# A transformer step on one Trainium2 core: modulation passes computed partly by GpSimd beside the FFN

## The reference, cut to what matters

```python
def modulation(cvec, w_mod, b_mod):              # w_mod: 1024 x 6144 for each layer
    m = jax.nn.silu(cvec) @ w_mod + b_mod
    return jnp.split(m, 6, axis=-1)              # shift, scale, gate, twice
def conv_ffn(h, w_in, conv_w, conv_b, w_out):    # d_ff = 2816
    u = h @ w_in
    up = jnp.pad(u, ((0, 0), (1, 1), (0, 0)))
    uc = up[:, :-2] * conv_w[0] + up[:, 1:-1] * conv_w[1] + up[:, 2:] * conv_w[2] + conv_b
    a, b = jnp.split(uc, 2, axis=-1)
    return (jax.nn.silu(a) * b) @ w_out
for i in range(4):
    # modulation(c_ctx, ...) for context tokens, modulation(c, ...) for latent tokens
    x = x + g1 * mixer(rmsnorm(x) * (1 + sc1) + sh1)
    x = x + g2 * conv_ffn(rmsnorm(x) * (1 + sc2) + sh2)
```

## Time and profile before

| what | value |
|---|---|
| median of three runs | 3136.57 us |
| the profiled execution, its own time | 3136.35 us |
| its span | 3134.6 us |
| PE busy | 3050.2 us, 97% |
| DVE busy | 2077.8 us, 66% |
| ACT busy | 1081.9 us, 35% |
| POOL busy | 404.3 us, 13% |
| granted TensorE clock, mean | 0.997 |

### The profile page before, as it was taken

The page is one execution under the profiler, slowest core; times in us unless marked ns, Lnnn a source line. Parts: engine busy times, 40 slices in busy tenths (PEclk is TensorE's granted clock), DMA queues, the critical chain, the costliest instruction groups (busy, mean ns, idle before and its releaser), DMA issues.

```text
span 3134.6 us, 55312 instructions
## 1 busy us (share of the span) xinstructions
PE 3050.2 (97%) x21670; PEld 2793.6 (89%) x21670; DVE 2077.8 (66%) x4004; ACT 1081.9 (35%) x2250; POOL 404.3 (13%) x392
## 2 busy tenths in 40 slices
PE   8999999999999999999999899999999989999999
PEld 6899999886699999998876699999998769999999
DVE  7766666777757666668657566656667775766665
ACT  3322223336633222324335432222223663422221
POOL 3000000133310000003237310000012231000000
PEclk9999999999999999999999999999999999999999
DMA  8533323110023332331200223233231002122211
GB/s 340 217 121 120 120 103 125 61 58 1 19 104 135 121 124 103 121 108 48 79 32 8 86 104 111 107 132 120 95 116 54 4 1 95 68 81 80 67 67 48
DMA packets 47202, 290.20 MB, mean 93 GB/s; under 512 B 4945, under 2 KB 11345, under 8 KB 13265
## 3 DMA queue, kind: packets, MB, share of 16 engines
q1 hardware_dynamic: 47058, 288.21, 25.4%
HBM read 283.98 MB, written 4.21 MB: 92 GB/s over the span
## 4 chain that ended last, share of the span: by engine, by line
PE 89%; DVE 5%; ACT 2%; DMA 2%; issue 1%; POOL 0%; SPq 0%; POOLq 0%; DVEq 0%; ACTq 0%
PE psA L2014 38%; PE psB L2014 24%; PE psA L2123 4%; PE psA L2124 3%; PE psA L2129 3%; PE psB L2031 2%; PE psB L741 2%; PE psA L811 2%; PE psA L2200 1%; DMA w_stage<-weights_dram 1%; PE psB L723 1%; PE psB L869 1%; PE psA L709 1%; PE psA L2205 1%; DVE top L1623 1%
## 5 line engine op out<-in xcount | busy, mean ns | idle before, releaser
L2014 PE MATMUL psA<-h_hi,w_hi 128*128 128x320 f32 (+1 forms) x2736 | 624.9, 310 | 2.5 <-ACT u_raw L2367 1.7
L2014 PE MATMUL psA<-h_lo,w_hi 128*128 128x320 f32 (+1 forms) x2720 | 620.4, 309 | 0.0
L2014 PE MATMUL psA<-h_hi,w_lo 128*128 128x320 f32 x2704 | 616.0, 309 | 0.0
L2554 DVE SCALAR_TENSOR_TENSOR xT<-psB,mod,xT 128x128 f32<-128x128 f32 x750 | 377.7, 546 | 221.6 <-PE psB L2014 221.6
L2014 PEld LDWEIGHTS psA<-h_hi,w_hi 128*128 128x128 f32 x2736 | 456.1, 188 | 4.2 <-ACT u_raw L2367 2.5
L2014 PEld LDWEIGHTS psA<-h_lo,w_hi 128*128 128x128 f32 x2720 | 455.1, 188 | 0.0
L2014 PEld LDWEIGHTS psA<-h_hi,w_lo 128*128 128x128 f32 x2704 | 452.1, 188 | 0.0
L2613 DVE TENSOR_SCALAR conv<-u_raw,vec_sb 128x642 f32<-128x642 f32 x176 | 108.3, 615 | 438.8 <-ACT u_raw L2367 438.8
L2431 DVE TENSOR_TENSOR w_lo<-w_stage,w_hi 128x512 fp32r<-128x512 f32 x496 | 353.0, 756 | 38.1 <-ACT w_hi L2282 38.0
L2014 PE MATMUL psB<-g_hi,wo_hi 128*128 128x320 f32 x1280 | 299.3, 315 | 0.1
L2014 PE MATMUL psB<-g_hi,wo_lo 128*128 128x320 f32 x1280 | 295.3, 312 | 0.0
(11 more groups left out here) (272 smaller groups left out, 4976.2 us busy)
## 6 DMA issues: line engine op xcount, KB each, us to landing
w_stage<-weights_dram SPq DMA_DIRECT2D x124, 1024.0 KB, 5.1
m_stage<-w_mod_dram SPq DMA_DIRECT2D x96, 1024.0 KB, 8.3
wo_stage<-w_out_dram SPq DMA_DIRECT2D x44, 1024.0 KB, 4.7
yT_dram<-xT SPq DMA_DIRECT2D x8, 322.0 KB, 2.2
xT<-xT_dram SPq DMA_DIRECT2D x1, 1544.0 KB, 9.8
xT<-xT_dram SPq DMA_DIRECT2D x1, 1032.0 KB, 6.3
w_stage<-weights_dram SPq DMA_DIRECT2D x2, 512.0 KB, 17.6
rope_raw<-rope_dram SPq DMA_DIRECT2D x3, 256.0 KB, 2.6
```

What stands on the lines that cost most here:

```text
L2014: ins = pe.matmul(o, wp, xp[:, a:b], start=first and n == 0, stop=last and n == 2)
L2554: ins = dve.scalar_tensor_tensor(out=xT[:, d, c:c + w], in0=tokens(ps, slot)[i], scalar=gate[:, d, i:i + 1], in1=xT[:, d, c:c + w], op0=AL ...
```

## The change

Passes 1 to 9 of layers 0 to 2 are divided between two engines. GpSimd takes six of the eight channels (k = 0 to 5) of m_stage: for each it multiplies the 2 x 256 weights of every partition with that partition's conditioning value, once for context and once for latent, and adds the products up in mod_acc. PE takes channels 6 and 7 as before, in the first two partition groups, and sums mod_acc over the partitions with `pick`, a matrix with one column of ones for each conditioning, into the other two groups. PE waits for GpSimd's last addition before each half (s_macc). GpSimd waits for both halves of m_stage, for the FFN norm's h (s_h), and from pass 2 on for PE's reading of the pass before. mod_acc and mod_prod lie where the norm's buffers are. The mask's semaphore is given up, its load counts on s_small.

```diff
+POOL_PASSES = 9
+POOL_KT = 6
+        mod_acc = [at(f"mod_acc{i}", [P, 2, 2 * P], F32, B_NORM + i * 2048) for i in range(2)]
+        mod_prod = [[at(f"mod_prod{k}{i}", [P, 2, 2 * P], F32, B_NORM + 4096 + (2 * k + i) * 2048) for i in range(2)]
+                    for k in range(2)]
+        pick = const("pick", [P, 2, 32])
-        s_mask = sem("mask_loaded")
+        s_macc = sem("mod_products_added")
-                dve.wait_ge(s_mask, 16)
+                dve.wait_ge(s_small, 64)
-                        sp.dma_start(mask_raw[:, :, :].rearrange("p a n -> p (a n)"), t["mask"]).then_inc(s_mask, 16)
+                        sp.dma_start(mask_raw[:, :, :].rearrange("p a n -> p (a n)"), t["mask"]).then_inc(s_small, 16)
+            # GpSimd
+            def mod_added(l, i):
+                for g in range(2):
+                    pool.wait_ge(s_m[0][g], i * 16 + 16 * (6 + MOD_PASSES * l + 1))
+                for k in range(POOL_KT):
+                    dst = mod_prod[k % 2] if k else mod_acc
+                    for c in range(2):
+                        w = m_stage[0][:, :, k, :]
+                        if k == 0 and c == 0:
+                            pool_own(pool.tensor_tensor(dst[c][:, :, :], w, cond[:, k, c:c + 1].unsqueeze(2)
+                                                        .to_broadcast([P, 2, 2 * P]), ALU.mult))
+                        else:
+                            pool_own(pool.tensor_scalar(dst[c][:, :, :], w, cond[:, k, c:c + 1], 1.0, ALU.mult, ALU.mult))
+                    for c in range(2 if k else 0):
+                        last = k == POOL_KT - 1 and c == 1
+                        pool.wait_ge(s_pown, pool_own.loop + (pool_own.n - (not last)))
+                        ins = pool.tensor_tensor(mod_acc[c][:, :, :], mod_acc[c][:, :, :], dst[c][:, :, :], ALU.add)
+                        if not last:
+                            pool_own(ins)
+                ins.then_inc(s_macc, 1)
+                if l < DEPTH - 1:                       # behind norm_pow(2 * l + 1)
+                    pool.wait_ge(s_h, KT * (2 * l + 1))
+                    mod_added(l, 1)
+                    ...
+                    with pool.Fori(2, POOL_PASSES + 1) as i:
+                        pool.wait_ge(s_mraw, i * 2 + 2 * MOD_PASSES * (l + 1))
+                        mod_added(l, i)
+            # PE
+            def mod_added(l, it, g):
+                pe.wait_ge(s_macc, it + POOL_PASSES * l)
+                for b, out in enumerate(beside(g)):
+                    n = slice(b * P, (b + 1) * P)
+                    for k in range(POOL_KT, KT):
+                        i = k - POOL_KT
+                        q = slice(32 * (i % 2), 32 * (i % 2 + 1))
+                        pe.matmul(out[q, :], cond[:, k, :], m_stage[0][:, g, k, n], start=(i < 2), stop=(k >= KT - 2))
+                    for c in range(2):
+                        q = slice(32 * (2 + c), 32 * (3 + c))
+                        ins = pe.matmul(out[q, :], pick[:, c, :], mod_acc[c][:, g, n], start=True, stop=True)
+                ins.then_inc(s_mraw, 1)
-                                mod_ffn(l, it + 1, d % 2)
+                                mod_added(l, it + 1, d % 2)
+            # DVE, at the start
+            own(dve.memset(pick[:, :, :], 0.0))
+            own.wait()
+            for c in range(2):
+                own(dve.memset(pick[:, c, c:c + 1], 1.0))
```

More of the change, by code:

```diff
@@ L173, in program @@
         xs = [at(f"xs{i}", [P, COLS], F32, B_NORM + (3 + i) * C) for i in range(2)]
+        mod_acc = [at(f"mod_acc{i}", [P, 2, 2 * P], F32, B_NORM + i * 2048) for i in range(2)]
+        mod_prod = [[at(f"mod_prod{k}{i}", [P, 2, 2 * P], F32, B_NORM + 4096 + (2 * k + i) * 2048) for i in range(2)]
+                    for k in range(2)]
+        assert 6 * 2048 <= 5 * C
         g_hi_last = at("g_hi_last", [P, 2, TOK], F32R, B_NORM + 5 * C + 4 * (NT + 4) * P)
@@ L2005, in _ @@
                 norm_pow(2 * l + 1)
+                if l < DEPTH - 1:
+                    pool.wait_ge(s_h, KT * (2 * l + 1))
+                    mod_added(l, 1)
+                    per = 4 * POOL_KT - 3
+                    own_before = pool_own.n
+                    with pool.Fori(2, POOL_PASSES + 1) as i:
+                        pool_own.loop = (i - 2) * per
+                        pool.wait_ge(s_mraw, i * 2 + 2 * MOD_PASSES * (l + 1))
+                        mod_added(l, i)
+                    assert pool_own.n - own_before == per
+                    pool_own.loop = 0
+                    pool_own.n = own_before + per * (POOL_PASSES - 1)
         @block.tensor
```

## The result

| | before | after |
|---|---|---|
| median of 4 runs each, beside each other | 3135.9 us (3134.7 to 3139.5) | 3269.8 us (3268.7 to 3282.0) |
| ratio, 95% interval | | 1.0433 [1.0418, 1.0447] |
| span of the profiled execution, mean granted clock | 3134.6 us, 0.997 | 3268.0 us, 0.982 |

The account below looks back on a forecast made before the run. PE, busy 97%, was taken as the bound. First passes 32 us plus 24 steady iterations x 2.8 = 67 us gave +99 on 3136.35 us: 3235 us; own range 3187 to 3280, with rivals 3120 to 3285.

Parts of the forecast that it names:

- its signs of being wrong: Iterations of 44.4 us with DVE unchanged, PE waiting for DVE's additions and hardly GpSimd, or passes of 25 us or less.
- The sum's mechanism: At tile 6 PE waits 3.1 us for GpSimd's late pass; the load loop keeps the lateness, period 47.5 us.
- rival 3: In the out product DVE is the new bound, its additions late: +4.5 us an iteration, 3279 us, chance 0.15.
- GpSimd's pass: GpSimd's multiplies and additions take 20.7 us alone plus 8.0 us lost to DVE, 28.7 us a pass.
- PE's saving: Each modulation half on PE has 8 matmuls in place of 16: 0.4 us less, 0.8 us a pass.
- First passes: In each layer's first iteration GpSimd has only 17.1 us: 3 x (28.7 - 17.1 - 0.8) = 32 us.
- The way back: From PE's tile 6 to GpSimd's next pass, through the next weight load: 19.6 us less the saving, 18.8 us.
- DVE's part: DVE's two-input operations wait for GpSimd's in the out product: +0.5 us an iteration, between +0 and +2.2.
- Clock loss: In the long first waits PE's clock may fall to 1.2 GHz: 1.7 us each, up to 5 us, left to the range.

Follow-up runs that it names:

- experiment 6: Changed kernel with the modulation weights loaded earlier and pass 1 of each layer on PE, GpSimd taking four channels instead of six: 3137.9 us, ratio 1.0004.
- experiment 4: Kernel with all eight channels on PE and GpSimd's result unused: GpSimd passes of 39 multiplies 3136.1 us, of 17 additions 3372.9 us.
- experiment 5: Changed kernel with the next modulation weights issued before the wait for w_out's split: 3219.2 us; with pass 1 of each layer also on PE 3188.7 us.

## Why the prediction was right in sign and low in size

Forecast 3235 us, measured 3270, inside the range; slower, as it said. But of its signs of being wrong one came true: in a steady iteration PE waits for DVE's additions and not for GpSimd (35.0 us in 6 waits, all in passes 1 to 3 of a layer). The iteration is 49.2 us and not 47 to 48.5. The sum's mechanism, PE at tile 6 waiting for GpSimd, is not what sets a steady iteration, and 3270 lies inside the range because the range took in rival 3.

- **GpSimd's pass.** Forecast 28.7 us, measured 28.6. On the page an addition takes 1669 ns (1267 alone by the earlier trace rows) and a later multiply 1039 (697 alone). The rows on contention were enough for this term.
- **PE's saving.** Forecast 0.4 us a half, measured 0.44. The reason given, half as many matmuls, held only because they are spread evenly over the column groups (experiment 6).
- **First passes.** Forecast 10.8 us each, measured 9.1 on average: the first pass took 26.2 us and not 28.7. Behind the wait of layer 1 the clock was 0.64 for 4.4 us, 1.6 us lost, which the text named and left to the range.
- **The way back.** Forecast 18.8 us from tile 6 to the next pass; measured 18.8 (1183.59 to 1202.4).
- **DVE's part: this step failed.** The text put +0.5 us on the loop, with +2.2 as the upper end, since "most of it passes while PE would wait for GpSimd anyway". Measured: PE reaches tile 6 1.8 us behind the end of the pass in a typical iteration, 18.8 + 28.6 + 1.8 = 49.2, and on average 4.46 over 45.2 a step, which is 2.2 over the 47.5. 24 x 1.66 = 40 us more, less 5 at the first passes and 4 behind pass 9, plus the 3.6 at the start, is the gap to 3270. What the working left out is what DVE brings with it: it took the addition of tile 0 as punctual, with 0.75 us of slack, and counted only what lies between the additions of tiles 0 and 3, which made DVE 1.5 us late at tile 5. Measured, tile 0 is added 3.3 us late, because a w_lo pair and a convolution step ahead of it are late already, and PE stands 2.5 to 2.7 us at tile 2. Clock loss stood in the text for the three long waits only; it came behind most of the short ones too, but one fall of it in a steady iteration adds nothing (49.14 against 49.12 us).
- **Rival 3** had the right mechanism and about the right time, 3279 us. The time is in part luck: its 4.5 us an iteration was not worked out from rows, and the 4.46 that met it is an average of 5.2 in a layer's first three steps and 4.0 in the others. Against it stood that at 50.56 DVE went first twice: that was a one-input multiply of GpSimd's, and experiment 4 shows that with these DVE pays seven times less than with additions. The evidence against it was from the wrong operation.

Open is whether DVE's 0.73 us for an addition comes from its length alone (1.27 us alone, against 0.70 for a multiply) or from its second input: the two were not varied apart.

## What to carry over

In this kernel DVE paid 0.73 us for each addition of 512 elements that GpSimd did beside it, and 0.1 us for each one-input multiply. Move multiplies, not sums; and count what DVE loses against its slack up to the point where the bounding engine needs it, what it loses ahead of that stretch included (here 5.5 us an iteration ahead of the out product were free, and 9 us left a step 4.5, 2.5 or 0.2 us longer than before by where they fell, PE's saving of 0.9 taken in). Whether a fall of the bounding engine's clock costs anything depends on what it would do next: 1.5 us of the iteration in experiment 5, nothing in the change itself, where PE would have waited for DVE again.

## What the runs showed of the hardware

- TensorE's granted clock fell to 1.2 GHz behind a wait of 2.63 us (0.53 over 3.5 us) and stayed at 2.4 GHz behind one of 2.50 us; in one kernel (experiment 5, pass 1 on PE) it fell behind a wait of 1.76 us and stayed behind another of 1.76 us. So the length of the wait alone doesn't say whether it falls.
- Powers of 8 elements took GpSimd 1.75 us each and cost DVE nothing (28.6 us an iteration in place of 28.5), where an addition of 1.67 us on average (experiment 4) cost it 0.73.
- f32 matmuls on 32 columns run beside each other in four column groups, and the three sets measured here last by their fullest group: 16 matmuls with four in each group 1.01 us, 12 with four in two groups and two in the others 1.00 us, 8 with two in each 0.58 us.
